# Taking the first four tiles of a feed-forward stage in two parts of 128 columns

## The reference

```
def rms_norm_2(x, gain=None):
    y = xf * lax.rsqrt(jnp.mean(xf * xf, axis=-1, keepdims=True) + EPS)
    if gain is not None:
        y = y * gain
def swiglu(h, w13, w2):
    gate, up = jnp.split(h @ w13, 2, axis=-1)
    return (jax.nn.silu(gate) * up) @ w2
# end of layer l in second_block
    x = x + rms_norm_2(cross_attention_2(h, m, cross_wq[l], cross_wkv[l], cross_wo[l]), cross_norms[l, 1])
    h = rms_norm_2(x, ffn2_norms[l, 0])
    x = x + 0.5 * rms_norm_2(swiglu(h, ffn2_w13[l], ffn2_w2[l]), ffn2_norms[l, 1])
```

## Time and profile before

| | |
|---|---|
| median of 3 runs | 2107.02 us (2104.38 to 2108.9) |
| profiled execution, its own time | 2113.54 us |
| its span | 2111.4 us |
| mean granted clock of TensorE | 0.991 of full |
| PE busy | 2047.4 us (97%) |
| DVE busy | 1364.5 us (65%) |
| ACT busy | 1093.1 us (52%) |
| DMA | 359.30 MB, mean 170 GB/s |

### The profile page before, as it was taken

One profiled execution on the slowest core, in us unless ns is written; L12 is line 12 of the kernel. 1 busy time (PEld: TensorE's weight loads), 2 busy tenths in 40 slices (PEclk: granted clock), 3 DMA queues, 4 the chain that ended last, 5 costly groups with the idle time before them and its releaser, 6 DMA issues.

```text
span 2111.4 us, 37767 instructions
## 1 busy us (share of the span) xinstructions
PE 2047.4 (97%) x15428; PEld 1903.2 (90%) x15428; DVE 1364.5 (65%) x1871; ACT 1093.1 (52%) x1702; POOL 51.4 (2%) x50
## 2 busy tenths in 40 slices
PE   7999999999999999999999999999999899998998
PEld 7989988999899889889888998999899898888997
DVE  6786866776566566767767554655477577756554
ACT  5846555554554454456456443644455455545443
POOL 0021000000000000010100000000000011000000
PEclk9999999999999999999999999999999999999999
DMA  7522454656465556434554655555555435544553
GB/s 260 166 78 81 160 183 146 202 186 191 155 220 187 188 173 200 165 111 140 180 200 143 207 181 189 197 182 181 189 181 180 155 111 169 167 164 152 184 184 120
DMA packets 98441, 359.30 MB, mean 170 GB/s; under 512 B 11160, under 2 KB 11480, under 8 KB 98008
## 3 DMA queue, kind: packets, MB, share of 16 engines
q1 hardware_dynamic: 98272, 356.90, 52.0%
HBM read 353.65 MB, written 1.05 MB: 168 GB/s over the span
## 4 chain that ended last, share of the span: by engine, by line
PE 79%; DVE 12%; ACT 6%; issue 2%; DMA 1%; SPq 0%; ACTq 0%; DVEq 0%
PE ps L920 14%; PE ps L922 14%; PE ps L921 14%; PE ps L985 6%; PE ps L987 6%; PE ps L986 6%; PE ps L908 5%; DVE wlo L1511 4%; PE ps L1064 2%; PE ps L1065 2%; PE ps L1071 2%; ACT whi L2220 2%; PE ps L954 1%; PE ps L953 1%; PE ps L952 1%
## 5 line engine op out<-in xcount | busy, mean ns | idle before, releaser
L1511 DVE TENSOR_TENSOR wlo<-raw,whi 128x1024 fp32r<-128x1024 f32 x635 | 772.1, 1225 | 504.9 <-ACT whi L2220 503.5
L2220 ACT ACTIVATE whi<-raw 128x1024 fp32r<-128x1024 f32 x635 | 665.1, 1056 | 394.1 <-PE ps L922 169.9
L920 PE MATMUL ps<-H,whi 128*128 128x256 f32 x2608 | 749.4, 287 | 1.7 <-DVE wlo L1511 1.3
L921 PE MATMUL ps<-L,whi 128*128 128x256 f32 x2608 | 740.7, 284 | 0.0
L922 PE MATMUL ps<-H,wlo 128*128 128x256 f32 x2608 | 740.6, 284 | 0.0
L920 PEld LDWEIGHTS ps<-H,whi 128*128 128x128 f32 x2608 | 502.7, 193 | 7.8 <-issue 4.5
L921 PEld LDWEIGHTS ps<-L,whi 128*128 128x128 f32 x2608 | 502.8, 193 | 0.6
L922 PEld LDWEIGHTS ps<-H,wlo 128*128 128x128 f32 x2608 | 502.5, 193 | 0.0
L987 PE MATMUL ps<-wlo,HH 128*128 128x512 f32 x440 | 173.7, 395 | 0.0
L985 PE MATMUL ps<-whi,HH 128*128 128x512 f32 x440 | 173.7, 395 | 0.0
L986 PE MATMUL ps<-whi,HL 128*128 128x512 f32 x440 | 173.7, 395 | 0.0
(11 more groups left out here) (422 smaller groups left out, 2974.4 us busy)
## 6 DMA issues: line engine op xcount, KB each, us to landing
raw<-in_ws SPq DMA_DIRECT2D x635, 512.0 KB, 3.6
prow<-in_rows SPq DMA_DIRECT2D x11, 512.0 KB, 6.6
row<-in_rows SPq DMA_DIRECT2D x9, 512.0 KB, 5.9
mema<-in_memT SPq DMA_DIRECT2D x4, 512.0 KB, 5.6
mema<-in_mem2T SPq DMA_DIRECT2D x4, 512.0 KB, 7.3
memb<-in_mem2T SPq DMA_DIRECT2D x4, 512.0 KB, 5.7
DT<-in_dec SPq DMA_DIRECT2D x2, 768.0 KB, 5.4
X<-in_x SPq DMA_DIRECT2D x1, 1024.0 KB, 9.8
```

Of the source, the lines that this page charges most:

```text
L920: e.matmul(o, h, hs[k], start=first and k == 0, stop=False, skip_group_check=True)
L921: e.matmul(o, h, ls[k], start=False, stop=False, skip_group_check=True)
L1511: e.tensor_tensor(m.wlo[:, n % SPL, :], r, h.bitcast(F32), SUB).then_inc(*c.lo.done(n))
L2220: e.activation(m.whi[:, n % SPL, :], m.raw[:, n % RAW, :], ACT.Copy).then_inc(*c.hi.done(n))
```

## The change

The junction to the last feed-forward, and only that one, gets four steps `half_head(..., part, 0)` ahead of the second turn (`jt`, `tb` = 1). They run all 96 matmuls of the head for rows 0 to 127, with 128 moving columns, into the first half of each tile's columns in the two held banks. The units aren't given back then. The head itself is replaced by four steps `half_head(..., part, 1)`, which run the 96 matmuls for rows 128 to 255 with the same weights and give the units back. The splits are placed anew: the fourth unit's ahead of part 3 of the first pass, and one more with each part of the second pass. Nothing else changes; each output element has the same products in the same order.

```
@@ junction @@
-            o.put("weights", n + 1 - sum(step[0] in ("keys", "values") for step in o.steps[begun:]))
+            o.put("weights", n + 1 - sum(step[0] in ("keys", "values", "half_head") for step in o.steps[begun:]))
...
             if fill:
                 later += o.few(fill - 1)
+            else:
+                for part in range(4):
+                    if part == 3:
+                        weights(4)
+                    o.put("half_head", ("fin", s), part, 0)
             o.put("jt", s, 1)
             o.put("jh", s, 1, 0)
-            weights(max(fill + 2, 4))
+            if fill:
+                weights(fill + 2)
             o.put("jh", s, 1, 1)
@@ ffn @@
-        head("fin", s)
+        if s == ("b", 1):
+            for part in range(4):
+                o.put("half_head", ("fin", s), part, 1)
+                o.put("weights", part + 2)
+        else:
+            head("fin", s)
@@ tensor_program @@
+    begun = {}
+
+    def half_head(stage, part, tb):
+
+        s, t = stage[1], slice(128 * tb, 128 * tb + 128)
+        if tb == 0:
+            if part == 0:
+                for j in range(2):
+                    bank_for(*stage, j, hold=True)
+            begun[stage, part] = [(k, n, tile(*fin_spec(s, n, k))) for k in (2 * part, 2 * part + 1) for n in range(4)]
+        rows = begun[stage, part]
+        if part % 2 == 0:
+            e.wait_ge(*act.after("h", s, tb, part // 2))
+        for k, n, i in rows:
+            h, lo = m.weight(i)
+            o = banks.of(*stage, n // 2)[:, (n % 2) * T:(n % 2 + 1) * T][:, t]
+            e.matmul(o, h, hs[k][:, t], start=tb == k == 0 and n % 2 == 0, stop=False, skip_group_check=True)
+            e.matmul(o, lo, hs[k][:, t], start=False, stop=False, skip_group_check=True)
+        if part % 2 == 0:
+            e.wait_ge(*dve.after("L", s, tb, part // 2))
+        for k, n, i in rows:
+            h, lo = m.weight(i)
+            o = banks.of(*stage, n // 2)[:, (n % 2) * T:(n % 2 + 1) * T][:, t]
+            mm = e.matmul(o, h, ls[k][:, t], start=False, stop=k == 7, skip_group_check=True)
+            names = [(*stage, n)] * (k == 7) + [("unit", i // UT)] * (i % UT == UT - 1)
+            if names and tb:
+                mm.then_inc(*pe.done(*names))
+        if tb and part == 3:
+            for j in range(2):
+                banks.release(*stage, j)
```

More of the change, by code:

```diff
@@ L1474, in branch_ready @@
         return [dve.after("yl", l, n, k // 2) for k in range(4)]
-    run = {"out_row": out_row, "tail": tail, "jt": turned_row, "head": head, "keys": keys, "mem_rms": mem_rms, "values": values, "mem_cols": mem_cols, "w1": w1,
+    run = {"out_row": out_row, "tail": tail, "jt": turned_row, "head": head, "half_head": half_head, "keys": keys, "mem_rms": mem_rms, "values": values, "mem_cols": mem_cols, "w1": w1,
            "kn": kn, "lora_up": lora_up, "px": in_tile("px", 14), "py": in_tile("py", 18), "gate1": in_tile("gate1", 22),
```

## The result

| | before | with the change |
|---|---|---|
| median | 2107.96 us (4 runs, 2104.38 to 2109.74) | 2131.05 us (4 runs, 2129.27 to 2132.01) |
| ratio | | 1.0109, 95% interval 1.0096 to 1.0123 |
| profiled execution, its span | 2113.54, 2111.4 us | 2131.45, 2129.3 us |
| mean granted clock | 0.991 | 0.984 |
| first turn to fifth tile | 22.97 us | 45.59 us |

The account below looks back on a forecast made before the run. TensorE was taken to bound the kernel: 4.0 us for the later fifth tile plus 0.9 for the clock made 4.9 us longer, 2107.0 to 2111.9 us, range 2102.5 to 2116.5.

Parts of the forecast that it names:

- What bounds the kernel: Whole kernel: TensorE, busy 2047.4 of 2111.4 us; any shift of the fifth tile's start moves the end by as much.
- The pace at 128 columns: Halved head products: starts 0.110 us apart, set by the weight load, against 0.120 us at 256 columns.
- Rival A: Halved head products: load hides, pace falls with columns to 0.064 us, 4.1 us faster; chance 0.10 for everything under 0.088.
- rival C: Halved head products: 128 columns run like plain fp32, 0.216 us each, 23 us longer, 2130 us; chance 0.17.
- The first half's gaps: First pass at the junction: PE idle 1.8 us and 1.4 us, the latter waiting for `L`.
- The added wait: Second turn queued behind all four parts, starting at 1920.8 instead of 1913.45; fifth tile 4.0 us later.
- The clock: Low granted clock at the junction: 0.9 us taken on top of 4.0, with 2.8 us in the slowest case.
- or if the clock stays low through the second part: Sign that the forecast is wrong: half clock in the second pass, adding up to 4 us more.
- The three cases of the clock: At the junction: stays full, nothing; falls and returns soon, some 0.3 us; returns after 5.9 us, 2.8 us.
- The covers: Weight units, splits and banks at the junction are ready in time and cost nothing; the fifth unit has 5.6 us cover.

Follow-up runs that it names:

- e1_mid: Kernel before, junction untouched; tiles 8 to 15 of the last feed-forward take 384 products of 128 columns instead of 192 of 256; 2126.51 against 2106.79 us.
- e2_wide: The change, but its first part streams its 128 columns twice and its second is the whole 256-column head, sums restarted; 2112.63 us against 2106.79 before the change.
- e6_change_filled: The change with its first part's two gaps filled by 7 and 4 unused products of 512 columns; 2113.56 us against 2108.58 before the change.
- e9_kick: The change plus 20 unused products of 512 columns ahead of part 1 of its first half; 2117.23 us against 2106.09 before the change.
- e3_redo: The change with its 128-column first part kept, but the whole 256-column head as second part, sums restarted; 2121.93 us against 2106.79 before the change.
- e4_part0: The change, but only part 0 of the head is halved, parts 1 to 3 keep 256 columns, splits placed as before; ratio 1.0010 to the kernel before.

## Why the prediction was wrong

*What bounds the kernel.* Right. Time that the traces show as added in or ahead of the dense stretch reached the end within the intervals: e1_mid's 384 x 0.1116 - 192 x 0.120 = 19.8 us as 19.7 (13 to 26), e2_wide's 5.8 as 5.8 (3.4 to 8.8). That they agree to a tenth is luck.

*The pace at 128 columns.* Right: 0.110 us from the loads, 0.111 to 0.112 measured at full clock. The rows bore it less firmly than the text says: the 0.33 us of the earlier trace rows run from the start of a product to the start of a load; from load to load (805.63 to 806.18, four of them) it is 0.14 each, and only the last two loads stand 0.11 apart. Halving the columns takes 7% off a product and not half. Rival A (0.064) and rival C (0.216 at full clock) are both out. C's total, 2130 us, nearly equals what was measured, and its step is wrong all the same: the pace of 0.213 is that of half clock.

*The first half's gaps.* Right: `H` 3.12 us behind the first turn (forecast 3.11), `L` part at 6.16 (forecast about 6.3).

*The added wait*, the second turn behind four parts: right as a mechanism, 4.0 us at full clock, 4.3 in e6_change_filled.

*The clock.* This is the step that failed, and it failed in its bound. I gave it 0.9 us with 2.8 at worst, from the one recovery at this junction that the trace of before shows, 5.9 us after the start of steady work. That recovery was under products of 256 columns, and I priced the return as if any dense stream gave it. The clock fell 5.3 us after the first turn and not 3.4, so that the 16 products ahead of the gap were spared, and then it did not come back until products of 256 columns ran. At half clock the 80 products behind the gap took 17.1 us for 8.9, the turn 1.76 for 1.35 and the second half 20.5 for 10.7, which is 18.5 us up to the fifth tile; its 18 first products took 1.7 us too much: 20 us, seven times my worst case. The text named it ("or if the clock stays low through the second part, which would add up to 4 us more"), with a size that is a fifth of it: it left out the first part and counted the second by less than half. The three cases of the clock had no row for 128 columns at half clock, so their upper end should have been all that follows the gap at half: (80 + 96) x (0.213 - 0.110) and 0.4 for the turn, 18.5 us. With the 4.0 that is 2129.5 us, inside the 2129.27 to 2132.01 that were measured.

*The covers.* Nothing of them was seen to fail: no wait for a weight unit or a bank stands among PE's waits of the change.

## What to carry to other kernels

Where work is cut into narrower products to fill a hole, price each at both clocks, and ask not only whether the hole lets the clock fall but whether the new products can win it back; if no row shows that, the bound is all of them at half clock. Look for the distance of two weight loads with full weights before halving the columns: here, 0.11 us, it was the floor, and half the columns saved 7% of a product. And a hole ahead of a dense stretch can cost the low clock behind it as well; 7 and 4 wide products on weights at hand were worth 5 us here, and moving real work into the hole a quarter of one.

## What the runs showed of the hardware

With fp32r operands and 128 x 128 weights, products stood 0.233 us apart at 512 columns, 0.120 at 256 and 0.112 at 128 at full clock, and 0.213 us apart at both 256 and 128 columns at half clock. What the granted clock did depended on where it stood: 43 us of 128-column products that started at full clock ran at full clock (e1_mid), while 37.5 us of the same products that started at half stayed at half (the change). It came back under 20 products of 512 columns (e9_kick) or under 4 to 22 of 256 (e3_redo, the change, e4_part0). I had expected neither. It fell in a gap of 1.1 us that followed one of 1.8 with 16 products of 128 columns between them, in the change, e3_redo, e4_part0 and e9_kick alike. On the pace at full clock the Trainium skill, "TensorE: Matmul & The Clock Gate", section LDWEIGHTS, agrees with 107 ns for a load of 128 columns; the 81 ns of its section Back-to-back issue gap did not hold for these operands, 112 ns measured.
